# A later modulation batch, a shorter group mask and a second bank for the first pair, in a two-layer backbone on one core

## The reference

```python
def layer(x, mod, P, l, ctx=None):
    sh1, sc1, g1, sh2, sc2, g2 = jnp.split(mod, 6, axis=-1)
    h = rms_norm(x, P["norm_attn_pre"][l]) * (1 + sc1) + sh1
    a, new_ctx = token_mix(h, P, l, ctx)
    x = x + g1 * rms_norm(a, P["norm_attn_post"][l])
    h = rms_norm(x, P["norm_ffn_pre"][l]) * (1 + sc2) + sh2
    x = x + g2 * rms_norm(moe(h, P, l), P["norm_ffn_post"][l])
    return x, new_ctx
# mod = silu(c) @ w_mod[l] + b_mod[l]        (6 x 1024 columns)
# in moe(), per token, 64 experts in 8 groups:
grp_score = jnp.sum(lax.top_k(grp, 2)[0], axis=-1)
_, gidx = lax.top_k(grp_score, TOPK_GROUPS)                      # 4 groups
emask = jnp.repeat(gmask, N_EXPERTS // N_GROUPS, axis=1) > 0
_, eidx = lax.top_k(jnp.where(emask, biased, NEG), TOP_K)        # 6 experts
# routed experts: silu(x Wg) * (x Wu), then Wd, times the gate; plus one shared expert
```

## Time and profile before

| | |
|---|---|
| median of 3 runs | 1789.97 us (1788.63 to 1791.96) |
| the profiled execution | 1792.57 us, its span 1791.0 us |
| PE busy | 1692.6 us, 95% |
| DVE, ACT, POOL busy | 439.3, 321.5, 116.8 us |
| transfers | 559.98 MB, mean 313 GB/s |

### The profile page before, as it was taken

How to read it: one execution, slowest core, us unless ns; L and a number is a source line. 1 busy time by engine, 2 the same in 40 slices (tenths; PEclk the granted TensorE clock), 3 DMA queues, 4 the chain that set the end, 5 groups by cost and what they waited for, 6 DMA issues and landing times.

```text
span 1791.0 us, 23175 instructions
## 1 busy us (share of the span) xinstructions
PE 1692.6 (95%) x8063; PEld 910.8 (51%) x8063; DVE 439.3 (25%) x1240; ACT 321.5 (18%) x754; POOL 116.8 (7%) x157
## 2 busy tenths in 40 slices
PE   4999999979999999999979999999699999999995
PEld 2877787533333333443358878784233333334432
DVE  2125444341111111111231444434311111111112
ACT  1010341111111111111110113302111111111111
POOL 3001000010000000001010000000100000000000
PEclk9999999989999999999989999899899999999998
DMA  9994223439999999999999622234599999999992
GB/s 350 418 373 150 95 95 124 159 138 375 419 419 419 419 420 419 420 419 414 414 366 369 240 104 98 91 112 176 210 413 420 420 419 420 420 420 419 419 417 96
DMA packets 87742, 559.98 MB, mean 313 GB/s; under 512 B 15916, under 2 KB 16064, under 8 KB 23120
## 3 DMA queue, kind: packets, MB, share of 16 engines
q1 hardware_dynamic: 72576, 528.51, 72.7%
q0 software_dynamic: 15056, 30.00, 4.9%
HBM read 575.95 MB, written 4.78 MB: 324 GB/s over the span
## 4 chain that ended last, share of the span: by engine, by line
PE 89%; DMA 5%; DVE 3%; issue 2%; ACT 1%; SPq 0%; DVEq 0%; POOL 0%; ACTq 0%; POOLq 0%
PE PS L974 24%; PE PS L580 13%; PE PS L997 12%; PE PS L1019 11%; PE PS L485 6%; PE PS L818 5%; PE PS L866 3%; DMA ring<-in_expert_blocks 3%; PE PS L531 2%; PE PS L598 2%; PE PS L645 2%; PE PS L904 2%; DMA ring<-in_blocks 1%; PE PS L804 1%; PE PS L708 1%
## 5 line engine op out<-in xcount | busy, mean ns | idle before, releaser
L974 PE MATMUL PS<-ring,region 128*64 128x512 f32 x2048 | 464.2, 598 | 1.9 <-ACT region L1239 1.7
L974 PEld LDWEIGHTS PS<-ring,region 128*64 128x64 f32 x2048 | 157.2, 138 | 297.4 <-issue 289.1
L580 PE MATMUL PS<-region,ring 128*128 128x256 f32 x1088 | 245.2, 382 | 0.0
L1019 PE MATMUL PS<-region 128*128 128x512 f32 x512 | 241.0, 594 | 0.0
L997 PE MATMUL PS<-ring,region 128*64 128x512 f32 x1024 | 233.9, 599 | 0.2
L580 PEld LDWEIGHTS PS<-region,ring 128*128 128x128 f32 x1088 | 204.0, 190 | 33.3 <-issue 6.3
L1655 DVE SCALAR_TENSOR_TENSOR region<-region,PS 128x256 f32<-128x256 f32 x64 | 27.0, 421 | 698.7 <-ACT region L1246 698.7
L485 PE MATMUL PS<-const,region 128*128 128x128 f32 (+1 forms) x925 | 142.2, 284 | 39.3 <-DMA region<-in_c 11.6
L485 PEld LDWEIGHTS PS<-const,region 128*128 128x128 f32 (+1 forms) x925 | 109.0, 144 | 137.0 <-issue 67.7
L997 PEld LDWEIGHTS PS<-ring,region 128*64 128x64 f32 x1024 | 67.8, 136 | 157.3 <-issue 156.7
L1250 ACT ACTIVATE region<-PS 128x512 f32<-128x512 f32 x128 | 76.4, 597 | 265.7 <-PE PS L997 265.7
(11 more groups left out here) (243 smaller groups left out, 1000.9 us busy)
## 6 DMA issues: line engine op xcount, KB each, us to landing
ring<-in_expert_blocks SPq DMA_DIRECT2D x384, 1024.0 KB, 18.3
ring<-in_blocks SPq DMA_DIRECT2D x120, 1024.0 KB, 13.3
region<-post_rows POOLq DMA_DIRECT2D x8, 512.0 KB, 4.7
h_table<-region POOLq DMA_DIRECT2D x4, 544.0 KB, 7.0
region<-in_w_kvk POOLq DMA_DIRECT2D x2, 640.0 KB, 14.8
region<-in_mla_w_ukv POOLq DMA_DIRECT2D x2, 512.0 KB, 18.0
region<-in_post_pack POOLq DMA_DIRECT2D x2, 512.0 KB, 21.1
region<-h_table,region POOLq DMA_INDIRECT x64, 8.2
```

The source lines that it names most:

```text
L580: last = pe.matmul(PS[:, j % 2, m * T:(m + 1) * T], w[:, k, m * P:(m + 1) * P], hT[:, k, :], start=(k == 0), stop=(k == KC - 1))
L974: last = pe.matmul(PS[e * CAP:(e + 1) * CAP, 0, :], xe[:, k, e * CAP:(e + 1) * CAP], w[:, k % 4, :], start=(k == 0), stop=(k == KC - 1), s ...
L1019: last = pe.matmul(PS[:, 4 + 2 * t + half, :], hot[:, t * P:(t + 1) * P], og[:, half * HALF:(half + 1) * HALF], start=False, stop=True, sk ...
```

## The change

1. Batch 5 of the modulation moves from the projections to the gap behind `shared_transposes(1)`, ahead of `shared_down(1)`. It writes bank 2. Its four loads move from ring places 28 to 31 to places 55 to 58, all in between move four places up, and the shared down weights come last (59). ACT copies the result (`late_staged`), and `down(0)` waits for that copy.
2. The bias and gain of g2 are loaded apart (`post_pack2`), and added and multiplied on POOL after the layer's last gather; POOL then writes `post_rows[1]` and calls `load_post(1)`, ahead of the next layer's parameter loads. DVE has two operations less.
3. The group mask takes one operation over the groups and one over the experts of each token tile: a value of 0 or 2e30, less 1e30, then the minimum with the biased score.
4. The second half of the first pair's inputs goes through bank 3, with no wait for ACT's copy of the first half.

```diff
@@ -63,9 +63,9 @@
-L_MOD = (0, 4, 10, 16, 22, 28)
-L_QA, L_KVA, L_QD, L_KD, L_QC, L_VD = (8, 9), 14, (15, 20), (21, 26), 27, (32, 33)
-L_GL01, L_UQ, L_GL, L_BR, L_OUT, L_SH = 34, 36, 37, 47, 53, 57
+L_MOD = (0, 4, 10, 16, 22, 55)
+L_QA, L_KVA, L_QD, L_KD, L_QC, L_VD = (8, 9), 14, (15, 20), (21, 26), 27, (28, 29)
+L_GL01, L_UQ, L_GL, L_BR, L_OUT, L_SH = 30, 32, 33, 43, 49, (53, 54, 59)
@@ -184,8 +184,10 @@
         gates = view(0, 24, T)
-        post_pack = view(0, 4, T)
-        post_sb = view(4 * T, 2, T)
+        post_pack = view(0, 2, T)
+        post_sb = view(4 * T, T)
+        post_pack2 = view(1024, 2, T)
+        post_sb2 = view(1536, T)
         w_kvk = view(2048, KC, KV_LORA + C_ROPE)
@@ -411,7 +415,7 @@
-        pool.dma_start(post_pack.rearrange("p k n -> p (k n)"), at_layer(a["post_pack"], l).rearrange("o p n -> p (o n)")).then_inc(post_in, 16)
+        pool.dma_start(post_pack.rearrange("p k n -> p (k n)"), at_layer(a["post_pack"], l)[:, :, 0:2 * T].rearrange("o p n -> p (o n)")).then_inc(post_in, 16)
@@ -420,7 +424,7 @@
         for g in range(MOD_BATCH):
-            pool.dma_start(post_rows[:, :, g * T:(g + 1) * T].rearrange("w t n -> t w n"), post_sb[32 * g:32 * g + 2]).then_inc(rows_out, 16)
+            pool.dma_start(post_rows[0, :, g * T:(g + 1) * T], post_sb[32 * g:32 * g + 2]).then_inc(rows_out, 16)
         pool.wait_ge(prep_ev, l * PREP_JOBS + 14)
@@ -442,9 +446,7 @@
         pool.memset(xg, 0.0).then_inc(xg_set, 1)
-        pool.wait_ge(x1_ready, (l + 1) * 2)
-        apart(pool)
-        load_post(1)
+        pool.dma_start(post_pack2.rearrange("p k n -> p (k n)"), at_layer(a["post_pack"], l)[:, :, 2 * T:4 * T].rearrange("o p n -> p (o n)")).then_inc(post_in, 16)
         pool.wait_ge(htok_ready, l * 4 + 4)
@@ -468,6 +470,19 @@
         pool.reg_add(passes, passes, npass)
+        pool.wait_ge(post_in, (l + 1) * 32)
+        pool.wait_ge(late_staged, l + 1)
+        apart(pool)
+        pool.tensor_tensor(post_sb2, post_sb2, post_pack2[:, 0, :], ALU.add).then_inc(late_sums, 1)
+        pool.wait_ge(late_sums, l * 2 + 1)
+        pool.tensor_tensor(post_sb2, post_sb2, post_pack2[:, 1, :], ALU.mult).then_inc(late_sums, 1)
+        pool.wait_ge(late_sums, l * 2 + 2)
+        apart(pool)
+        for g in range(MOD_BATCH):
+            pool.dma_start(post_rows[1, :, g * T:(g + 1) * T], post_sb2[32 * g:32 * g + 2]).then_inc(late_rows, 16)
+        pool.wait_ge(late_rows, (l + 1) * MOD_BATCH * 16)
+        apart(pool)
+        load_post(1)
     pool.wait_ge(state_out, DEPTH * 6 * 16)
@@ -523,19 +538,23 @@
             group, half = divmod(batch, 2)
+            bank = 2 if batch == 5 else MOD_BANK[group]
+            at = 0 if batch == 5 else half * 256
             for g in range(MOD_BATCH):
...
                     w = slot_cols(L_MOD[batch] + g, 256)
-                    last = pe.matmul(PS[32 * g:32 * g + 32, MOD_BANK[group], half * 256:half * 256 + 256], condT[:, k, :], w[:, k, :],
+                    last = pe.matmul(PS[32 * g:32 * g + 32, bank, at:at + 256], condT[:, k, :], w[:, k, :],
                                      start=(k == 0), stop=(k == KC - 1), skip_group_check=True)
...
                         release(last, frees)
-                    if k == KC - 1 and (half == 0 or g < 3):
+                    if k == KC - 1 and (batch in (0, 2) or g < 3):
                         release(last)
-            if half:
+            if batch in (1, 3, 4):
                 last.then_inc(mod_done, 1)
+            elif batch == 5:
+                last.then_inc(late_done, 1)
@@ -633,9 +652,9 @@
         mod_transposes(1, (2, 3))
-        project(6, L_KD[1], 0)
-
-        def project_rows(j, n):
+        project(6, L_KD[1])
+
+        def project_rows(j, n, releases=1):
@@ -644,7 +663,7 @@
                                      start=(k == 0), stop=(k == KC - 1))
-                    if t == 0 and k == 0:
+                    if t == 0 and k == 0 and releases:
                         release(last)
@@ -661,8 +680,7 @@
         last.then_inc(z_done, 1)
-        mod_batch(5)
-        project_rows(Z_VD, L_VD[0])
+        project_rows(Z_VD, L_VD[0], 0)
         mod_transposes(2, (0, 1))
@@ -900,8 +918,8 @@
                 if t == 0 and k % 4 == 0:
-                    arrived(L_SH + k // 4)
-                last = pe.matmul(PS[:, 2 + t, :], h2T[:, k, t * P:(t + 1) * P], wide(L_SH + k // 4)[:, k % 4, :],
+                    arrived(L_SH[k // 4])
+                last = pe.matmul(PS[:, 2 + t, :], h2T[:, k, t * P:(t + 1) * P], wide(L_SH[k // 4])[:, k % 4, :],
                                  start=(k == 0), stop=(k == KC - 1))
@@ -913,16 +931,18 @@
-        def shared_down(t):
+        def shared_down(t, frees=0):
             if t == 0:
-                arrived(L_SH + 2)
+                arrived(L_SH[2])
             pe.wait_ge(shid_ready, l * 2 + t + 1)
...
                     last = pe.matmul(PS[:, 4 + 2 * t + half, :], shid[:, f, t * P:(t + 1) * P],
-                                     down_slot(L_SH + 2)[:, f, half * HALF:(half + 1) * HALF],
+                                     down_slot(L_SH[2])[:, f, half * HALF:(half + 1) * HALF],
                                      start=(f == 0), stop=(f == 1), skip_group_check=True)
+                    if frees and half == 0 and f == 0:
+                        release(last, frees)
             return last
@@ -950,7 +970,8 @@
         shared_transposes(1)
-        release(shared_down(1))
+        mod_batch(5)
+        release(shared_down(1, frees=1))
         pe.wait_ge(npass_ready, l + 1)
@@ -990,6 +1011,8 @@
                     pe.wait_ge(og_ready, done + 2 * g)
+                else:
+                    pe.wait_ge(late_staged, l + 1)
                 for half in range(2):
@@ -999,13 +1022,14 @@
             def transpose_inputs(g, half, frees=0):
+                bank = 3 if g == 0 and half else 1
                 if half == 0:
                     pe.wait_ge(xg_in[g % XG], pe_gathers[g % XG] + 16 * (g // XG + 1))
-                if g >= 1 or half:
+                if g >= 1:
...
                 for c in range(4):
-                    last = transpose(PS[:, 1, c * P:(c + 1) * P], xg[:, g % XG, (4 * half + c) * P:(4 * half + c + 1) * P])
+                    last = transpose(PS[:, bank, c * P:(c + 1) * P], xg[:, g % XG, (4 * half + c) * P:(4 * half + c + 1) * P])
                     if c == 0 and frees:
@@ -1093,7 +1117,8 @@
             act.wait_ge(mod_done, l * 3 + group + 1)
-            act.activation(mod_rows[:, group, :], bank((1, 5, 6)[group]), ACT.Copy).then_inc(mod_staged, 1)
+            n = 256 if group == 2 else 512
+            act.activation(mod_rows[:, group, 0:n], bank((1, 5, 6)[group])[:, 0:n], ACT.Copy).then_inc(mod_staged, 1)
@@ -1225,6 +1250,8 @@
         take_shared(1)
+        act.wait_ge(late_done, l + 1)
+        act.activation(post_sb2, bank(2)[:, 0:T], ACT.Copy).then_inc(late_staged, 1)
         act.wait_ge(npass_ready, l + 1)
@@ -1236,7 +1263,7 @@
                 act.wait_ge(xe_tr, done + (2 * g + half + 1))
-                act.activation(xe[:, 4 * half:4 * half + 4, :].rearrange("p k s -> p (k s)"), bank(1), ACT.Copy).then_inc(xe_ready, 1)
+                act.activation(xe[:, 4 * half:4 * half + 4, :].rearrange("p k s -> p (k s)"), bank(3 if g == 0 and half else 1), ACT.Copy).then_inc(xe_ready, 1)
@@ -1418,15 +1445,10 @@
         ve.scalar_tensor_tensor(out=pre2[:], in0=modT[:, 32:40, :], scalar=1.0, in1=gain(56), op0=ALU.add, op1=ALU.mult).then_inc(mod_ready, 1)
-        dve.wait_ge(post_in, (l + 1) * 16)
-        dve.wait_ge(mod_staged, l * 3 + 3)
-        for i in range(2):
-            step(ve.tensor_tensor(post_sb[:, i, :], mod_rows[:, 1 + i, i * T:(i + 1) * T], post_pack[:, 2 * i, :], ALU.add))
-            ins = ve.tensor_tensor(post_sb[:, i, :], post_sb[:, i, :], post_pack[:, 2 * i + 1, :], ALU.mult)
-            if i == 0:
-                step(ins)
-            else:
-                ins.then_inc(post_sums, 1)
+        dve.wait_ge(post_in, l * 32 + 16)
+        dve.wait_ge(mod_staged, l * 3 + 2)
+        step(ve.tensor_tensor(post_sb, mod_rows[:, 1, 0:T], post_pack[:, 0, :], ALU.add))
+        ve.tensor_tensor(post_sb, post_sb, post_pack[:, 1, :], ALU.mult).then_inc(post_sums, 1)
         dve.wait_ge(lam_exp, l + 1)
@@ -1588,15 +1610,11 @@
         dve.wait_ge(vector_step, step.base + step.n)
-        step(ve.tensor_scalar(r_gm, r_grep[:, :, 0:8], FAR / 2, None, ALU.is_ge))
-        grouped = [P, 2, N_GROUPS, 8]
+        step(ve.tensor_scalar(r_gm, r_grep[:, :, 0:8], FAR / 2, 2e30, ALU.is_ge, ALU.mult))
         for t in range(2):
-            step(ve.tensor_tensor(r_mask[:, t, 0:N_EXPERTS].rearrange("p (g k) -> p g k", g=8), r_bias[:, t, :].rearrange("p (g k) -> p g k", g=8),
-                                  per_column(r_gm[:, t, :], grouped[0:1] + grouped[2:], 2), ALU.mult))
-        step(ve.tensor_scalar(r_gm, r_gm, 1e30, -1e30, ALU.mult, ALU.add))
-        for t in range(2):
```

(13 more changed lines are left out.)

## The result

The changed kernel takes **1794.64 us** (median of 8 runs, 1793.55 to 1796.19), the kernel before 1790.3 us beside it (8 runs, 1787.04 to 1792.65): a ratio of 1.0029, with a 95% interval of 1.0019 to 1.0039. It is slower, by 4.3 us. The forecast was 1793.8.

A forecast was written before the change was run, and what follows sets the result against it. PE was taken as the bound, transfers in the last third of each layer's experts. -7.2 - 1.9 + 8.1 + 4.8 = +3.8 us moved the median from 1789.97 to 1793.8; range 1783 to 1797.5, the forecast's own 1791 to 1797.

The forecast's parts named there:

- Batch 5 out of the projections: In the projections, where PE is always busy, removing the batch saves 3.59 us a layer, -7.2 for both.
- The batch in the gap costs nothing: Between shared expert and first pair, PE does the batch's 3.59 us while waiting for DVE's lists, 2.0 us left: cost nothing.
- The second bank: From the first gathered rows' transposes to the first gate-up: 0.96 us saved a layer, -1.9 for both.
- The mask, 0: In DVE's routing: `sel` comes earlier but PE takes it up no sooner, so 0 saved, at most 0.1.
- The gather behind the ring loads: Ahead of the first pair: the gather takes 7.9 us behind five loads, 4.4 and 3.7 more by layer, +8.1 together.
- rival 2: At the first gather: it only shares transfer engines with ring loads, late by 1.3 us; time 1788.3, chance 0.08.
- g2's rows: At each layer's end: their 1.05 MB stand ahead of ring loads PE awaits, 2.4 us a layer, +4.8 for both.
- The batch's own 4 MB are no such cost: In the gap: the batch's loads move into an almost silent stretch, and the ring is full by the first pair.
- rival 5: In the gap: PE works to 387.2 and might keep 2.4 GHz, saving 3.5 us per layer; time 1786.8, chance 0.05.
- What was to show it: In the new profile: projections 3.6 us sooner, about 400 GB/s from 386 to 398 us, first gather landing after 7.9 us.

The follow-up runs named there:

- Run 9: The changed kernel with the two loads of g2's rows moved behind the layer's last expert load, no ring loads held: 1787.97 us, ratio 0.9988 to the kernel before.
- Run 5: The changed kernel with all five loads of the freed slots held until PE takes up the first gathered rows: 1791.57 us, ratio 1.0011 to the kernel before.

## Why the prediction was right

Forecast and result agree within 1 us, and its main steps stand, though by sizes that partly cancel.

- *Batch 5 out of the projections*, -3.6 a layer: right. `project_rows` starts at 116.77 us instead of 120.92. PE was 0.5 us earlier ahead of this place already; 3.6 are the batch's.
- *The batch in the gap costs nothing:* right, PE still waits 1.21 us for the lists, and 0.85 in the second layer. The cover is nearly used up: what goes there beyond that would show.
- *The second bank*, -0.96: right, 0.95.
- *The mask, 0:* mis-sized. The forecast priced it by DVE's lead ahead of `sel`, and missed that DVE reads the pass count behind it. With it alone the kernel was 0.9991 of before, about 1.6 us (0.2 to 3.2 by the interval), of which the trace shows 0.7 at the first gate-up. In the changed kernel the lists come 1.1 and 0.6 us sooner behind `sel`. How much of either is the mask's is not shown, since the register load shrank too.
- *The gather behind the ring loads*, +4.4 and +3.7: right in kind, as three loads held show, +4.8 and +4.4 by landing. What the runs changed is the how. The forecast took 7.9 us from the fourth gather, "behind all of them" and in "the same queue". It is not the same queue (q0 and q1), and a line behind all of them would make each load ahead cost 2.5 us; one load fewer gave 0.2 and 1.0. So the size came out by a likeness and not by the mechanism. The queues do take turns, as rival 2 had it, but rival 2's 1.3 us was far too small. It was also worked out from 0.56 MB for one gather, where the trace shows 0.55 MB for the first three; with a third of that it would have been 0.4 us.
- *g2's rows*, +2.4 a layer: right, +3.0 and +2.3 in the long gate-ups. Run 9 took them away and 6.7 us went, 5.0 of them in these two gate-ups.
- *"The batch's own 4 MB are no such cost":* this holds in the changed kernel, because its ring is full before the first pair. Run 5 shows what it would be: 2 of these 5 loads, made later, cost 4 us a layer.
- *The clock staying up* (rival 5): it did not, 0.50 from 384.3 to 401.3 us, and 386.4 to 403.5 before.

What was to show it did, on a clock that is 5.8 us earlier at this place (`sel`). The batch was put at 379.9 and stands at 374.05; the loads were to be freed from 383.5 to 387.2 and were issued from 377.9 to 381.5; they were to be under way until 398.4, and 400 GB/s end at 393.

That the sum came within 1 us is partly luck: the stretches before `sel` and the lists behind it gave a little that was not counted, and the gather and the rows took a little more.

## What to carry to other kernels

Work moved into a stretch where its engine waits is free for that engine, but look at what its end releases: here five weight loads were let go just ahead of a small gather on which PE waited 10 us, and with it every pair of experts. Hold back as many as bring the small transfer through, and not more, where the stage behind goes at the pace of the transfers: here three of five gained 11 us and all five 3. In such a stage 1.05 MB ahead of the last load cost 2 to 2.6 us a layer, at its end and at its front alike; free were only the silent stretch, as long as nothing else used it, and the place behind the last load. Where one execution of each kernel is compared, split it by stage and set low-clock stretches apart first: the spans here differed by 0.6 us and the medians by 4.3.

## What had not been expected of the hardware

- A gather of some 0.18 MB (0.55 MB for the first three) on POOL's queue, issued 3 to 7 us behind five loads of 1.05 MB on SP's, landed after 8.3 us for 3.5, though the queues are not the same; with four loads ahead it took 8.1, with two 3.5. Its first packet comes 4 us or more after the issue, about 1.5 in silence.
- The load of one register on DVE's queue (the number of passes) took from 0.33 to 1.79 us in these runs, with the lists behind it.
- The clock's stretch at 0.50 goes with the waits around the lists and the gather together. The kernel before, with waits of 5.31 and 5.12 us, and the changed one, with 1.21 and 9.97, both stood at 0.50 for 17 us and had first gate-ups of 9.44 and 9.90 us. With three or five loads held and a wait of 5.2 us for the gather it was 10 us, and the gate-ups took 8.65 and 8.91.
